# The output gate's columns inside the DeltaNet group passes of a decoder layer

## The reference, cut to what matters

```python
q, k, v = split(silu(causal_short_conv(dn_qkv)))        # by head
o = gated_delta_rule(q, k, v, g, beta)                  # chunks of 64, a triangular inverse in each
y_b = rms_norm(o, dn_out_norm) * silu(dn_z)
merged = sigmoid(gate_a) * (y_a @ w_branch_a) + sigmoid(gate_b) * (y_b @ w_branch_b)
x = x + merged @ w_out
```

## Time and profile before

| | us |
|---|---|
| median of 3 runs (1897.95 to 1900.97) | 1899.73 |
| profiled execution, its own time | 1897.58 |
| its span, first to last instruction | 1895.8 |
| mean granted PE clock, share of full speed | 0.989 |
| PE busy / DVE / ACT / POOL in the span | 1834.5 / 1202.7 / 905.8 / 251.0 |

### The profile page before, as it was taken

How to read it: one execution, slowest core, us unless ns; L and a number is a source line. 1 busy time by engine, 2 the same in 40 slices (tenths; PEclk the granted TensorE clock), 3 DMA queues, 4 the chain that set the end, 5 groups by cost and what they waited for, 6 DMA issues and landing times.

```text
span 1895.8 us, 30416 instructions
## 1 busy us (share of the span) xinstructions
PE 1834.5 (97%) x10842; PEld 1604.8 (85%) x10842; DVE 1202.7 (63%) x1424; ACT 905.8 (48%) x1043; POOL 251.0 (13%) x371
## 2 busy tenths in 40 slices
PE   7879999999999999999999999999999999999996
PEld 5768888787888888888888888888888888888885
DVE  5767867775566656566567655565556555555676
ACT  5544544444455545545444544444444444434453
POOL 4050614225000000000001000000000000000034
PEclk9989999999999999999999999999999999999998
DMA  6343444436445565655655555555555555565653
GB/s 222 104 139 113 136 138 136 128 126 199 134 162 193 183 199 173 199 191 182 194 188 178 190 194 192 178 187 190 193 183 184 194 187 194 173 204 176 195 175 106
DMA packets 103102, 327.42 MB, mean 173 GB/s; under 512 B 23088, under 2 KB 23216, under 8 KB 103024
## 3 DMA queue, kind: packets, MB, share of 16 engines
q1 hardware_dynamic: 89024, 321.43, 51.2%
q10 hardware_dynamic: 13632, 3.67, 0.9%
q0 software_dynamic: 368, 1.31, 0.2%
HBM read 323.23 MB, written 3.15 MB: 172 GB/s over the span
## 4 chain that ended last, share of the span: by engine, by line
PE 79%; issue 11%; POOL 6%; DVE 2%; ACT 1%; DMA 0%; ACTq 0%; POOLq 0%; DVEq 0%; SPq 0%
PE acc L281 49%; PE acc L286 25%; POOL blk_t L463 2%; POOL blk_x L465 2%; PE acc L302 1%; PE acc L303 1%; PE acc L304 1%; POOL sqsum L445 1%; ACTq L1048 0%; ACT ax L942 0%; ACT whi L266 0%; POOLq L417 0%; PE ps L601 0%; DVE wlo L274 0%; POOL invT L472 0%
## 5 line engine op out<-in xcount | busy, mean ns | idle before, releaser
L274 DVE TENSOR_TENSOR wlo<-raw,whi 128x1024 fp32r<-128x1024 f32 x604 | 752.0, 1265 | 419.6 <-ACT whi L266 409.6
L281 PE MATMUL acc<-ax,whi 128*128 128x512 f32 x3328 | 846.6, 396 | 9.7 <-ACT whi L266 9.6
L266 ACT ACTIVATE whi<-raw 128x1024 fp32r<-128x1024 f32 x604 | 623.0, 1054 | 454.1 <-PE acc L286 421.7
L281 PEld LDWEIGHTS acc<-ax,whi 128*128 128x128 f32 x3328 | 602.8, 190 | 122.5 <-issue 12.3
L286 PEld LDWEIGHTS acc<-ax,wlo 128*128 128x128 f32 x3328 | 454.4, 190 | 33.4 <-DVE wlo L274 0.5
L286 PE MATMUL acc<-ax,wlo 128*128 128x256 f32 x3328 | 464.1, 282 | 0.0
L281 PE MATMUL acc<-fx,whi 128*128 128x512 f32 x704 | 176.3, 392 | 0.0
L281 PEld LDWEIGHTS acc<-fx,whi 128*128 128x128 f32 x704 | 126.6, 189 | 22.6
L504 POOL TENSOR_TENSOR sqsum<-sqsum,t 128x512 f32<-128x512 f32 x16 | 22.1, 1380 | 804.5 <-ACT t L1196 804.5
L931 ACT ACTIVATE t<-acc 128x512 f32<-128x512 f32 x96 | 57.3, 597 | 146.7 <-PE acc L286 146.7
L1297 DVE TENSOR_TENSOR t<-acc,t 128x512 f32<-128x512 f32 x96 | 66.3, 690 | 88.2 <-ACT t L931 87.8
(11 more groups left out here) (247 smaller groups left out, 1356.3 us busy)
## 6 DMA issues: line engine op xcount, KB each, us to landing
raw<-in_win SPq DMA_DIRECT2D x224, 512.0 KB, 3.6
raw<-in_wgu SPq DMA_DIRECT2D x176, 512.0 KB, 4.4
raw<-in_wd SPq DMA_DIRECT2D x88, 512.0 KB, 4.2
raw<-in_wb SPq DMA_DIRECT2D x32, 512.0 KB, 4.2
raw<-in_wo SPq DMA_DIRECT2D x32, 512.0 KB, 4.4
raw<-in_wpg SPq DMA_DIRECT2D x32, 512.0 KB, 3.5
raw<-in_wa SPq DMA_DIRECT2D x16, 512.0 KB, 5.3
xT<-in_xT SPq DMA_DIRECT2D x4, 512.0 KB, 6.7
```

The costliest lines, as they stand in the source:

```text
L266: nc.scalar.activation(whi[:, s], raw[:, s], ACT.Copy).then_inc(hi_done, 1)
L274: nc.vector.tensor_tensor(wlo[:, s], raw[:, s], whi[:, s].bitcast(F32), ALU.subtract).then_inc(lo_done, 1)
L281: nc.tensor.matmul(o, whi[:, s, kt, m * P:(m + 1) * P], x[:, k].rearrange("p q n -> p (q n)"), start=begin, stop=False, skip_group_check=True)
```

## The change

z's columns are no longer a phase. Each group has 32 halves: k, q, v, and the 8 halves of the same four heads' z. z's two blocks of a group are evacuated into those heads' place in `oT`, scaled there by `R` and put through SiLU (`silu_z0` at step 29, `silu_z1` at step 1 of what follows). `o_gain` multiplies the outputs by the gain and by what stands in `oT`. `yb`'s high and low parts are made in `uv`, four heads at a time.

The tables change with it. `conv_b(2,2)`, `make_qkT`, `silu_v`, `transpose_v` and `scale_v` are steps 24 to 27 of the own group; they were steps 0 to 5 of the next. `g_rows` goes from step 2 to 1, `g_copy` and `store_x` to step 2 with `g_copy` ahead, and `transpose_v` no longer waits for the next `gb`. `LAST` is gone: `uv` uses `FINISH`, three steps earlier. In group 0 several steps shift, and `beta_g` on ACT and `sum_g` on DVE are issued behind the group's stages. `gmw`, `gmb` and `praw` have other places in SBUF, and POOL loads them at other points.

Left out below are the renaming of "qkv" to "qkvz" and the removed z loops of PE and SP.

```diff
-GH = 6 * HID
+GH = 8 * HID
...
-PLAN = [("qkv", NGROUPS, GH, (3, 3)), ("uv", 1, 2 * HWIDE + 4 * HID, (3, 3)), ("z", 2, 4 * HID, (2, 2)),
+PLAN = [("qkvz", NGROUPS, GH, (4, 4)), ("uv", 1, 2 * HWIDE + 4 * HID, (3, 3)),
...
-    gmw = shared("gmw", [P, GMT, P], F32, 62)
-    gmb = shared("gmb", [P, GMT, P], F32, 66)
+    gmw = shared("gmw", [P, GMT, P], F32, 24)
+    gmb = shared("gmb", [P, GMT, P], F32, 36)
...
+    praw = t[1][:, 0:PLE // P]
...
+            w_in_block("qkvz", 0, BLK_Z, 3 * HWIDE)
...
+                w_in_block("qkvz", g, BLK_Z + g, 3 * HWIDE)
...
-            pool.wait_ge(x_stored, 64 * NGROUPS)
+            pool.wait_ge(vT_out, NGROUPS)
             pool.dma_start(gmw[:], gmw_d).then_inc(gm_in, 16)
-            pool.dma_start(gmb[:].rearrange("p g n -> p (g n)"), gmb_d.to_broadcast([P, GM])).then_inc(gm_in, 16)
-
-            pool.wait_ge(merge_out, 4 * NGROUPS - 3)
-            pool.wait_ge(diag_turned, NGROUPS)
-            pool.dma_start(praw[:], pT_d).then_inc(p_in, 16)
-            pool.wait_ge(gm_in, 32)
+            pool.wait_ge(k_rows_out, NGROUPS)
+            pool.dma_start(praw, pT_d).then_inc(p_in, 16)
+            pool.wait_ge(delta_out, 5 * NGROUPS - 1)
+            pool.dma_start(gmb[:].rearrange("p g n -> p (g n)"), gmb_d.to_broadcast([P, GM])).then_inc(gm_bias_in, 16)
+            pool.wait_ge(gm_in, 16)
...
-                    pe.wait_ge(qkT_done, g)
+                    pe.wait_ge(v_scaled, 2 * g)
...
-                pe.wait_ge(g_copied, last_rows(d))
...
-                pe.wait_ge(v_scaled, 2 * d + 2)
+                if not isinstance(d, int):
+                    pe.wait_ge(g_copied, d + 2)
...
-            FINISH = {4: transpose_v, 5: merge32_a, 6: merge32_b, 7: merge64_a, 8: merge64_b, 9: first_tile, 10: carry,
+            FINISH = {5: merge32_a, 6: merge32_b, 7: merge64_a, 8: merge64_b, 9: first_tile, 10: carry,
                       11: second_tile, 12: outputs, 13: o_columns, 14: o_row}
-            LAST = {4: transpose_v, 8: merge32_a, 9: merge32_b, 10: merge64_a, 11: merge64_b, 12: first_tile, 13: carry,
-                    14: second_tile, 15: outputs, 16: o_columns, 17: o_row}
-            FIRST = {12: k_columns, 13: k_rows, 15: g_rows, 16: gram_m, 18: transpose_k, 22: q_gram_columns}
-            START = {2: g_rows, 11: k_columns, 12: k_rows, 14: gram_m, 17: transpose_k, 21: q_gram_columns}
+            FIRST = {12: k_columns, 13: k_rows, 16: g_rows, 17: gram_m, 19: transpose_k, 22: q_gram_columns, 26: transpose_v}
+            START = {1: g_rows, 11: k_columns, 12: k_rows, 14: gram_m, 17: transpose_k, 21: q_gram_columns, 26: transpose_v}
...
+            def z_part(b, g):
+
+                low_part("qkvz", g, (7 + b) * HID, b, tiles(oT, 2 * g + b))
...
+            def silu_z(b, g):
+
+                act.wait_ge(z_scaled, 2 * g + b + 1)
+                carry_wait(act)
+                z = tiles(oT, 2 * g + b)
+                f(z, z, ACT.Silu).then_inc(z_silu, 1)
...
-            FINISH = {2: (silu_v,), 3: (store_x,), 4: (load_diag,), 6: (copy_p32,), 7: (copy_inv,), 10: (copy_v0,), 12: (copy_v1,),
+            FINISH = {1: (silu_z1,), 2: (store_x,), 3: (load_diag,), 6: (copy_p32,), 7: (copy_inv,), 10: (copy_v0,), 12: (copy_v1,),
                       13: (square_o,), 14: (o_rt,)}
-            LAST = {2: (silu_v,), 5: (store_x,), 6: (load_diag,), 9: (copy_p32,), 10: (copy_inv,), 13: (copy_v0,), 15: (copy_v1,),
-                    16: (square_o,), 17: (o_rt,)}
-            FIRST = {11: (silu_k,), 13: (k_root,), 15: (g_copy,), 16: (decay_m,), 17: (store_m, g_exp, decay_q), 18: (load_m,), 20: (silu_q,)}
-            START = {3: (g_copy,), 10: (silu_k,), 11: (decay_m,), 12: (k_root,), 15: (store_m,), 16: (load_m,), 18: (silu_q,), 19: (g_exp, decay_q)}
+            FIRST = {11: (silu_k,), 13: (k_root,), 17: (g_copy,), 18: (decay_m,), 20: (store_m,), 21: (load_m, silu_q),
+                     23: (g_exp, decay_q), 25: (silu_v,), 29: (silu_z0,)}
+            START = {2: (g_copy,), 10: (silu_k,), 11: (decay_m,), 12: (k_root,), 15: (store_m,), 16: (load_m,), 18: (silu_q,),
+                     20: (g_exp, decay_q), 25: (silu_v,), 29: (silu_z0,)}
...
-                if n == 11:
-                    beta_g()
-                if n == 13:
+                if n == 14:
                     tails()
-                if n == 14:
+                if n == 15:
                     tok_exp()
                 for stage in FIRST.get(n, ()):
                     stage(0)
+                if n == 11:
+                    beta_g()
...
+                    for stage in START.get(n, ()) if n < 5 else ():
+                        stage(g)
                     for stage in FINISH.get(n, ()):
                         stage(g - 1)
-                    for stage in START.get(n, ()):
+                    for stage in START.get(n, ()) if n >= 5 else ():
...
+            def yb_high(d):
+
+                act.wait_ge(ps_free, NGROUPS + 1)
+                f(ybhi[:, 4 * d:4 * d + 4], oT[:, 4 * d:4 * d + 4], ACT.Copy).then_inc(yb_hi, 1)
...
+                if n in (19, 21, 23, 25):
+                    yb_high((n - 19) // 2)
...
-                for b in range(4):
-                    split("z", i, b * HID, (b + 1) * HID)
-                    low_part("z", i, (b + 1) * HID, b % 2, piece(t[0], b % 2))
-                    act.wait_ge(z_scaled, 4 * i + b + 1)
-                    f(piece(t[0], b % 2), piece(t[0], b % 2), ACT.Silu).then_inc(z_silu, 1)
-                    act.wait_ge(z_gated, 4 * i + b + 1)
-                    f(tiles(ybhi, 4 * i + b), piece(t[1], b % 2), ACT.Copy).then_inc(yb_hi, 1)
...
+                dst = piece(pre, p % 2)[:, :, 4:] if p < 6 else tiles(oT, 2 * g + p - 6)
+                sum_parts("qkvz", 8 * g + p, p % 2, dst)
+
+            def scale_z(p, g):
+
+                z = tiles(oT, 2 * g + p - 6)
+                v.tensor_tensor(z, z, over(R[:], 2), ALU.mult).then_inc(z_scaled, 1)
...
-                v.tensor_scalar(oT[:, ds(GROUP * d, GROUP)], psv[1], cols[:, C_DNO:C_DNO + 1], None, ALU.mult).then_inc(o_gained, 1)
+                dve.wait_ge(z_silu, 2 * d + 2)
+                o = oT[:, ds(GROUP * d, GROUP)]
+                v.scalar_tensor_tensor(o, psv[1], cols[:, C_DNO:C_DNO + 1], o, ALU.mult, ALU.mult).then_inc(o_gained, 1)
...
-            FINISH = {0: (make_qkT, conv_b(2, 2)), 5: (scale_v, turn_diag), 7: (copy_invT32,), 8: (copy_p64,),
+            FINISH = {5: (turn_diag,), 7: (copy_invT32,), 8: (copy_p64,),
                       9: (copy_invT64,), 10: (copy_nwT,), 11: (copy_state,), 13: (o_gain,), 14: (o_inv, o_diagonal), 15: (norm_o,)}
-            LAST = {0: (make_qkT, conv_b(2, 2)), 5: (scale_v,), 8: (turn_diag,), 10: (copy_invT32,), 11: (copy_p64,),
-                    12: (copy_invT64,), 13: (copy_nwT,), 14: (copy_state,), 16: (o_gain,), 17: (o_inv, o_diagonal), 18: (norm_o,)}
-            FIRST = {11: (select_heads,), 13: (k_mean, k_diag), 14: (norm_k,), 16: (diff_m, make_negm), 17: (diff_q,),
-                     20: (scale_k,), 21: (decay_q,), 23: (q_mean,)}
+            FIRST = {11: (select_heads,), 13: (k_mean, k_diag), 14: (norm_k,), 18: (diff_m,), 19: (make_negm,), 21: (scale_k, diff_q),
+                     23: (q_mean,), 25: (make_qkT,), 26: (decay_q,), 27: (scale_v,)}
             START = {0: (select_heads,), 10: (diff_m,), 12: (k_mean, k_diag), 13: (norm_k,), 15: (make_negm,), 17: (diff_q,),
-                     18: (scale_k,), 20: (decay_q,), 22: (q_mean,)}
-            FIRST_CONV = {8: conv_a(1, 0), 9: conv_b(1, 0), 14: conv_a(0, 1), 18: conv_b(0, 1), 22: conv_a(2, 2)}
-            CONV = {5: conv_a(1, 0), 8: conv_b(1, 0), 13: conv_a(0, 1), 16: conv_b(0, 1), 21: conv_a(2, 2)}
+                     18: (scale_k,), 22: (q_mean, decay_q), 25: (make_qkT,), 27: (scale_v,)}
+            FIRST_CONV = {8: conv_a(1, 0), 9: conv_b(1, 0), 15: conv_a(0, 1), 17: conv_b(0, 1), 22: conv_a(2, 2), 24: conv_b(2, 2)}
+            CONV = {5: conv_a(1, 0), 8: conv_b(1, 0), 14: conv_a(0, 1), 16: conv_b(0, 1), 21: conv_a(2, 2), 24: conv_b(2, 2)}
...
+                if n == 13:
+                    sum_g()
...
+            def yb_low(d):
+
+                dve.wait_ge(yb_hi, d + 1)
+                v.tensor_tensor(yblo[:, 4 * d:4 * d + 4], oT[:, 4 * d:4 * d + 4], ybhi[:, 4 * d:4 * d + 4].bitcast(F32),
+                                ALU.subtract).then_inc(yb_lo, 1)
...
+                if n in (20, 22, 24, 26):
+                    yb_low((n - 20) // 2)
```

More of the change, by code:

```diff
@@ L77 @@
 E0, _e = {}, 0
-for _name, _n in (("qkv", 6 * NGROUPS), ("uv", 4), ("z", NB), ("mix", 4 * NB), ("ffn", 2 * FB), ("ple", NB)):
+for _name, _n in (("qkvz", 8 * NGROUPS), ("uv", 4), ("mix", 4 * NB), ("ffn", 2 * FB), ("ple", NB)):
     E0[_name] = _e
@@ L205, in build @@
     acc_read = [sem(f"acc_read{n}") for n in range(2)]
-    cols_in, x_in, ba_in, gm_in = sem("cols_in"), [sem(f"x_in{n}") for n in range(4)], sem("ba_in"), sem("gm_in")
```

(49 more changed lines are left out.)

52 lines of the change are left out of this document (28 added, 24 removed).

## The result

The changed kernel takes **1886.17 us** (median of 4 runs, 1886.01 to 1888.21) against 1899.32 before in the same comparison: a ratio of 0.9933 [0.9921, 0.9946]. The forecast was 1881.3, with a range of 1868 to 1894. The gain is 13.2 us where 18.4 were forecast: the direction and the main mechanism are right, 5 us are missing. The profiled execution took 1886.01 us, its span is 1884.1, 11.7 less than before.

The account below looks back on a forecast made before the run. PE, busy 97% of the span, was taken as the bound, so only its idle time and slow stretches could move. Terms -24.8 + 4.4 + 2.8 - 3.1 + 0.3 + 2 = -18.4 gave 1881.3 us, range 1868 to 1894.

Parts of the forecast that it names:

- The inversion's wait, -24.8: Transposes of v no longer wait for gb behind POOL's inversion: 18.5 us of waits and 6.3 of slow PE go.
- z's halves inside the groups, 0: z's 32 halves enter the groups at the same 2.79 us each, their evacuations covered: 0.
- transpose_v, +4.4: At transpose_v after half 26, PE waits 1.1 us for DVE's conv and qkT in each of four groups: +4.4 us.
- g_rows, +2.8: g_rows one half earlier waits 1.4 us for DVE's head selection in groups 2 and 3: +2.8 us.
- Rival C: Slow clock follows each of seven new waits, 2.1 us each, 14.7 more: 1896 us; chance 0.04.
- o_row, -3.1: conv_a(0,1) goes behind o_diagonal on DVE, so PE's three 1.1 us waits at o_row nearly go: -3.1 us.
- uv, +0.3: In uv, merge64_b and its copy meet the late split: new wait 2.0 us, old 1.7, so +0.3.
- Group 0, +2: k_columns' wait moves to k_rows (6.5 us for 5.3), transpose_k about 3.0 late, kbeg's 1.9 goes: +2 us.
- Rival A: All waits dissolve, DVE ahead at step 24 and group 0's waits gone: -35 us, 1864.5; chance 0.12.
- B: DVE's last quarter is the new bound, transpose_v 2.8 us later in four groups: 1892.5 us; chance 0.20.
- D: POOL's inversion is still last, store_x holds ACT's splits: 1914.5 us, slower; chance 0.06.

Follow-up runs that it names:

- experiment 2: The changed kernel with g_copy behind store_x again on ACT, z's halves staying in the groups: 1884.52 us, 0.9923.
- experiment 5: The changed kernel with transpose_v one half later (step 27) and scale_v at step 28: 1876.52 us, 0.9884.
- experiment 4: The changed kernel with beta_g ahead of the stages again and sum_g at step 12 in group 0: 1887.74 us, 0.9934.
- experiment 10: The kernel of experiment 8 with, in uv, copy_p64 ahead of that half's late split on DVE: 1863.48 us, 0.9808.
- experiment 1: The kernel before with only g_copy put ahead of store_x on ACT, z staying a phase of its own: 1895.95 us, 0.998.
- experiment 8: The changed kernel with the four edits of experiment 3, experiment 5, experiment 6 and experiment 7 together: 1866.81 us, 0.9836.
- experiment 6: The changed kernel with beta_a and beta_g two halves earlier and sum_g at step 12 in group 0: 1880.27 us, 0.9911.
- experiment 3: The changed kernel with g_rows at step 2 and g_copy at step 3 again in groups 1 to 3: 1881.01 us, 0.9903.
- experiment 7: The changed kernel with transpose_k and conv_b(0,1) one step later in group 0: 1880.47 us, 0.9901.
- experiment 9: The changed kernel run again without an edit: 1885.84 us, 0.9926.

## Why the prediction was right, and where its sizes were not

1. **The inversion's wait, -24.8: right.** Group 1 shows -12.0 for -12.1, and the slow stretches of the three waits are gone with them (granted clock 1.00, 0.99, 0.99). The chain was read rightly down to its cure: POOL's inversion ends ahead of ACT's store_x by 5 us and more. The working named both distance and order; by experiment 2 the order is not needed. That the distance alone, without the transposes' move, would do it is argued from the trace and was not run.
2. **z's halves inside the groups, 0: right** within the 0.8 us behind uv. No wait for whi or wlo stands within a group, and o_gain takes 1.27 us with the third operand as without it.
3. **transpose_v, +4.4:** measured 4.8 of wait, 5.7 with what goes with it (experiment 5).
4. **g_rows, +2.8: the size was off.** Each wait is 0.83 us, shorter than the 1.4 estimated, since DVE's turn took 2.48 us here and 2.97 in the earlier trace rows. But a slow half of about 1.5 us stands behind each, and the term is 4.6. Rival C had this mechanism and put it down for all seven waits; it holds for these two of the seven, not for the transposes or the merge.
5. **o_row, -3.1: right.** Its line is gone from the list, -3.4.
6. **uv, +0.3: the sign was off.** The new wait is 2.2 against 2.0 forecast, but uv became 1.3 us shorter, the transposes' 0.8 apart. The old wait of 1.6 had a slow stretch behind it, which the term left out: from merge32_b (L703) to merge64_a (L715) it is 5.89 us there (462.61 to 468.50) and 4.38 between the same two steps of the changed kernel (530.66 to 535.04), 1.5 less. PE's timeline of the kernel before, behind that wait:

```profile
464.19 0.80 PE L302 MATMUL acc<-whi,ax 128*128 128x512 f32 x1
...
465.64 0.63 PE L302 MATMUL acc<-whi,ax 128*128 128x512 f32 x1
```

The same matmuls of the changed kernel behind its wait of 2.2:

```profile
542.40 0.50 PE L303 MATMUL acc<-whi,ax 128*128 128x512 f32 x1
...
543.20 0.40 PE L303 MATMUL acc<-whi,ax 128*128 128x512 f32 x1
```

7. **Group 0, +2: the step that failed**, measured +6.1 (8.2 less the transposes and their wait, 2.1). The wait at k_rows was 6.39 for 6.5, and experiment 4 confirms that it was only moved. The rest was mis-sized: transpose_k was put at "about 3.0 us late" with no slow stretch behind it, and it is 4.1 us and 2.7 of slow PE. This is the largest miss, and it is one of method: the wait of the same length was charged with its slow stretch in part 1, not here. These are 3.8 of the 4.1 missed. The rest nearly cancels: the half behind sum_squares (half 6) is slow in this profile and costs 1.6 (it comes and goes without an edit ahead of it, last section), and the slow stretch behind k_rows, put down as "the same", is some 1.6 shorter than the one that stood behind k_columns.

Rival A (all waits dissolve) gave 1864.5, and experiment 10 takes 1863.5. That they are so near is in part luck: experiment 10 still waits 2.98 us at k_rows and 0.5 to 1.0 at three other places of group 0, and it saves slow halves that A's sum didn't hold. B (another half late in four groups) and D (inversion still last) didn't occur: POOL's chain takes 36 us as before.

By stages, the misses are +4.3 (group 0), +0.1, +1.2 and +1.2 (groups 1 to 3), -1.6 (uv) and +1.6 (0.8 of scatter at the start, 0.8 behind uv with no cause found): 6.8 us by these rounded figures, from -18.6 to the span's -11.7. That the median misses by only 4.9 is luck: the forecast added 2.15 for the medians' distance from the profiled execution, which the kernel before had, and in the changed kernel it is 0.16. The forecast of the profiled execution itself, 1879.2, is 6.8 below the measured 1886.01.

## What to carry to other kernels

A chain of fixed length on a slow engine (here 36 us on POOL) is hidden by distance in the work of the bounding engine. Freeing one consumer by the order in a queue only moved the wait to the next one here (experiment 1, 4 of 13 us). When a stage moves by a step, each wait that results is charged with the slow stretch that can stand behind it, as the removed ones are. Then read the list of waits of the result: most of the remaining ones here went with one changed key in a table, and the prices, each read at its own place in the trace, added up (experiment 8).

## What the runs showed of the hardware that was not expected

- A wait of 0.70 to 1.04 us ahead of g_rows' eight matmuls on 16 partitions had a slow half behind it (2.8 to 3.7 us for 2.1) at 13 of the 14 such places in seven profiles; the one without is group 3 of experiment 5. The same matmuls without a wait (group 1) and 128-row transposes behind a longer wait, 1.2 us, ran on at a granted clock of 1.00. What parts them stays open, and it isn't the shape of the matmuls alone: behind one and the same wait of 0.82 us at k_columns, with the same 128-row matmuls, the granted clock was 0.74, 0.59 and 1.00 in experiments 6, 8 and 10.
- Behind one and the same wait of 1.8 to 2.1 us in group 0 (sum_squares, L553) the high matmuls of the next half took 2.2 us in six profiles (the kernel before, experiments 2, 3, 5, 6, 10) and 3.2 to 3.8 in six (the changed kernel, experiments 1, 4, 7, 8, 9), though no edit of an experiment stands ahead of it. With the 0.8 us by which the launch's first half varies, this makes the 2.2 us by which single edits can't be told apart by time alone; the cause stays open.
- DVE pauses 2.3 to 3.2 us ahead of its first split where its hardware loop turns (groups 2 and 3), in all twelve profiles. For 20 of these 24 turns the trace shows no wait; for the other four it names ACT's whi (2.31 to 2.39 us), which in all four had ended 3 us before. Group 1, entered from the written-out group, has no such pause.
